# Routing of a mixture of experts moved between the tiles of the cross-attention's output projection, in a one-layer encoder

## The reference

```python
h = h + memory_cross_attention(rms_norm(h, norm_xatt), rms_norm(mem, mem_norm), wq, wk, wv, wo)  # 4 heads of 128
hn = rms_norm(h, norm_moe)
cl = hn @ w_coarse + b_coarse                    # 4 groups, the best one is taken
p_g, g = top_k(softmax(cl), 1)
top_v, top_i = top_k((hn @ w_fine)[group g] + b_fine, 2)   # 2 of its 8 experts
gate = softmax(top_v) * p_g
y = sum over the chosen experts e of (silu(hn @ w_gate[e]) * (hn @ w_up[e]) * gate) @ w_down[e]
out = rms_norm(h + y, final_norm)
```

## Time and profile before

| | us |
|---|---|
| median of three runs | 2049.28 |
| the profiled execution | 2048.28 |
| its span, first to last instruction | 2046.2 |
| PE, DVE, ACT, POOL busy in the span | 1825.2, 486.6, 398.4, 58.1 |
| DMA over the span | 247 GB/s |

### The profile page before, as it was taken

One profiled execution on the slowest core, in us unless ns is written; L12 is line 12 of the kernel. 1 busy time (PEld: TensorE's weight loads), 2 busy tenths in 40 slices (PEclk: granted clock), 3 DMA queues, 4 the chain that ended last, 5 costly groups with the idle time before them and its releaser, 6 DMA issues.

```text
span 2046.2 us, 29333 instructions
## 1 busy us (share of the span) xinstructions
PE 1825.2 (89%) x11998; PEld 1329.1 (65%) x11998; DVE 486.6 (24%) x1120; ACT 398.4 (19%) x1071; POOL 58.1 (3%) x100
## 2 busy tenths in 40 slices
PE   3999999999999999999769888999888899988882
PEld 3888888899988884467467554556555455655541
DVE  1101333777777741011320000000000000000003
ACT  2112221355555540012210000000000000000001
POOL 0000000000000000000000000000000000000000
PEclk9999999999999999999869999999999999999996
DMA  8832352200000045353218999999999999999993
GB/s 293 157 103 88 107 187 83 83 2 1 0 0 0 0 158 203 134 205 152 101 79 346 430 431 428 432 430 422 429 432 424 428 422 431 418 430 433 423 422 147
DMA packets 93357, 505.87 MB, mean 247 GB/s; under 512 B 39188, under 2 KB 43656, under 8 KB 74872
## 3 DMA queue, kind: packets, MB, share of 16 engines
q1 hardware_dynamic: 85456, 487.62, 58.7%
q0 software_dynamic: 6848, 14.12, 2.3%
q10 hardware_dynamic: 1000, 3.37, 0.6%
HBM read 498.76 MB, written 18.91 MB: 253 GB/s over the span
## 4 chain that ended last, share of the span: by engine, by line
PE 65%; DMA 27%; DVE 3%; ACT 2%; issue 1%; SPq 1%; DVEq 0%; ACTq 0%; POOLq 0%
DMA ring<-in_wu 26%; PE ps L1592 14%; PE ps L1233 13%; PE ps L1489 5%; PE ps L1406 4%; PE ps L1425 3%; PE ps L1631 3%; PE ps L1507 3%; PE ps L1582 3%; PE ps L1381 1%; PE ps L1431 1%; PE ps L1548 1%; PE ps L1516 1%; SPq L267 1%; PE ps L1213 1%
## 5 line engine op out<-in xcount | busy, mean ns | idle before, releaser
L1592 PE MATMUL ps<-ring,rkv 128*64 128x256 f32 x4096 | 477.0, 393 | 65.2 <-DMA ring<-in_wu 38.4
L1592 PEld LDWEIGHTS ps<-ring,rkv 128*64 128x64 f32 x4096 | 325.3, 142 | 226.2 <-DMA ring<-in_wu 49.6
L1233 PE MATMUL ps<-hnT,ring 128*128 128x256 f32 (+1 forms) x1280 | 282.2, 379 | 2.2 <-PE ps L1233 1.0
L1233 PEld LDWEIGHTS ps<-hnT,ring 128*128 128x128 f32 (+1 forms) x1280 | 239.1, 187 | 47.7 <-issue 10.2
L1631 PE MATMUL ps<-ring,gg 128*64 128x512 f32 x1024 | 240.1, 623 | 30.2 <-DMA ring<-in_wd 20.6
L1631 PEld LDWEIGHTS ps<-ring,gg 128*64 128x64 f32 x1024 | 83.3, 143 | 165.0 <-issue 141.7
L1177 DVE SCALAR_TENSOR_TENSOR gg<-ps,tmp,gg 128x256 f32<-128x256 f32 x32 | 15.5, 484 | 515.0 <-PE ps L1592 515.0
L1582 PE MATMUL ps<-hnT,sw 128*128 (+1 forms) x1024 | 120.8, 280 | 7.4 <-DVE hnT L1161 7.4
L1582 PEld LDWEIGHTS ps<-hnT,sw 128*128 128x128 f32 x1024 | 117.7, 195 | 13.3 <-issue 13.3
L1406 PE MATMUL ps<-ring 128*128 128x128 f32 x768 | 114.6, 275 | 0.1
L1406 PEld LDWEIGHTS ps<-ring 128*128 128x128 f32 x768 | 100.3, 192 | 0.7 <-ACT ring L558 0.3
(11 more groups left out here) (316 smaller groups left out, 1710.3 us busy)
## 6 DMA issues: line engine op xcount, KB each, us to landing
ring<-in_wg SPq DMA_DIRECT2D x32, 4096.0 KB, 20.1
ring<-in_wu SPq DMA_DIRECT2D x32, 4096.0 KB, 22.2
ring<-in_wd SPq DMA_DIRECT2D x32, 4096.0 KB, 18.0
ring<-in_w_in SPq DMA_DIRECT2D x7, 4096.0 KB, 15.1
ring<-in_w_out SPq DMA_DIRECT2D x4, 4096.0 KB, 13.9
ring<-in_w_in SPq DMA_DIRECT2D x16, 512.0 KB, 7.5
ring<-in_xatt_wk SPq DMA_DIRECT2D x1, 4096.0 KB, 13.5
ring<-in_xatt_wv SPq DMA_DIRECT2D x1, 4096.0 KB, 13.5
```

The lines of the kernel that those rows point to most:

```text
L1233: ins = mm(ps[0:rows_, m % 2, 0:T], lhs, hnT[:, k, :], start=k == 0, stop=k == KD - 1)
L1592: ins = mm(ps[CAP * h:CAP * h + CAP, bank, 0:T], xT[:, k, CAP * i:CAP * i + CAP], slot_k(slot)[:, k, T * h:T * h + T], start=k == 0, stop= ...
```

## The change

- Cross-attention goes head by head: the queries of head f are followed by the scores of head f - 1, the turning of head f - 2 and the values of head f - 3, two PSUM banks for each step. The output projection's first three tiles begin with the heads that are ready.
- Between the projection's tiles PE turns the rows of `tokA` as they are, unnormalised, and makes their logits four feature tiles at a time. The squares are taken by tiles of 512 too. The gain of `norm_moe` is multiplied into the router's weights; the row's 1/rms scales the logits when DVE reads them.
- The group and the experts are chosen by rank: how many others are larger (or equal and earlier), all pairs compared at once. The masks are built before the weights, so the counts run while the weights are made.
- The one-hots of experts 0 and 1 come before the loop, the others inside it.
- `select` reads raw rows of `tokA` with a step of 16 elements as the stationary operand. DVE evicts with the gain (`x_out` was ACT's). The row's 1/rms goes into the table as a third column: it scales the Silu's input and is part of the gate weight.
- `norm_moe` is one more row among the parameters and a small load by features; its broadcast load goes.

```diff
-ID, BO, MK, SU, ON, IO, SM, TV, DI, HB = 0, 128, 256, 768, 896, 1024, 1088, 1344, 1348, 1356
-NCST = 1357
-
-P_MIX, P_XATT, P_MEM, P_SP, P_SN = 0, 16, 32, 64, 94
+ID, BO, MK, SU, ON, IO, SM, TV, LT, HB, TH = 0, 128, 256, 768, 896, 1024, 1088, 1344, 1348, 1412, 1413
+NCST = 1417
+
+P_MIX, P_XATT, P_MEM, P_MOE, P_SP, P_SN = 0, 16, 32, 48, 64, 94
...
-    c[:, DI:DI + 8] = np.arange(8, 0, -1)
+    c[:, LT:LT + 64] = np.tri(8, k=-1).reshape(1, 64)
+    c[:, TH:TH + 4] = CAP * np.arange(4) - (np.arange(4) == 0)
...
-        xpT = hnT[:, 0:8, :].rearrange("p (h b) t -> p h b t", b=2)
-
-        gain_moe = memtok[:, 0, :]
+        xpT = sw[:, 0].rearrange("p (h b) t -> p h b t", b=2)
...
-        tab = tmp[:, 1400:1400 + 2 * NE].rearrange("p (j v) -> p j v", v=2)
+        tab = tmp[:, 1400:1400 + 3 * NE].rearrange("p (j v) -> p j v", v=3)
+        gain_moe = tmp[:, 1504:1504 + KD]
+        sqp = st[:, 40:48]
...
-            todo = [(0, r, by(a[name], P)) for r, name in ((P_MIX, "norm_mix"), (P_XATT, "norm_xatt"), (P_MEM, "mem_norm"))]
+            todo = [(0, r, by(a[name], P)) for r, name in ((P_MIX, "norm_mix"), (P_XATT, "norm_xatt"), (P_MEM, "mem_norm"), (P_MOE, "norm_moe"))]
...
-            for dst, g in ((gain_moe, "norm_moe"), (gain_fin, "final_norm")):
-                pool.dma_start(dst, bass.AP(tensor=a[g].tensor, offset=0, ap=[[0, P], [1, D]])).then_inc(S["gain_in"], 16)
+            pool.dma_start(gain_fin, bass.AP(tensor=a["final_norm"].tensor, offset=0, ap=[[0, P], [1, D]])).then_inc(S["gain_in"], 16)
             pool.wait_ge(S["xs_tr"], 4)
-            pool.dma_start(wr[:, :, 0:NG], a["wc"].rearrange("(p k) n -> p k n", p=P)).then_inc(S["route_in"], 16)
-            pool.dma_start(wr[:, :, NG:NR], a["wf"].rearrange("(p k) n -> p k n", p=P)).then_inc(S["route_in"], 16)
+            pool.dma_start(wr[:, :, 0:NG], a["wc"].rearrange("(k p) n -> p k n", p=P)).then_inc(S["route_in"], 16)
+            pool.dma_start(wr[:, :, NG:NR], a["wf"].rearrange("(k p) n -> p k n", p=P)).then_inc(S["route_in"], 16)
+            pool.dma_start(gain_moe, a["norm_moe"].rearrange("(p k) -> p k", p=P)).then_inc(S["route_in"], 16)
...
@@ scalar @@
+            for f in range(XH + 1):
+                if f < XH:
+                    queries(f)
+                if f >= 1:
+                    exp_head(f - 1)
+                if f >= 2:
+                    head_turned(f - 2)
+                if f >= 3:
+                    head_out(f - 3)
+            head_out(XH - 2)
+            head_turned(XH - 1)
+            head_out(XH - 1)
...
+            def row_squares(n):
+                b, q = n // 4, slice(F * (n % 4), F * (n % 4) + F)
+                act.wait_ge(S["xw_add"], n + 1)
+                A(tokB[:, b, q], tokA[:, b, q], ACT.Square, accum_out=sqp[:, n:n + 1]).then_inc(S["sq_done"], 1)
+
+            def rows_turned(n, c0=0):
+                act.wait_ge(S["r_tr"], n + 1)
+                b, k, bank = n // 4, 4 * (n % 4) + c0, TR_BANK[n] + c0 // 2
+                src = ps[:, bank, P * c0:4 * P].rearrange("p (k t) -> p k t", t=P)
+                A(hnT[:, k:k + 4 - c0, P * b:P * b + P], src, ACT.Copy).then_inc(S["r_ev"], 1)
+
+            def row_std(b):
                 act.wait_ge(S["var_done"], 5 + b)
                 A(stat(3, 2)[:, b:b + 1], stat(3, 1)[:, b:b + 1], ACT.Sqrt).then_inc(S["std_done"], 1)
-            turned(3)
+
+            row_squares(0)
+            row_squares(1)
+            for n in range(2, 7):
+                row_squares(n)
+                rows_turned(n - 2)
+                if n == 4:
+                    row_std(0)
+            rows_turned(5)
+            rows_turned(6)
+            row_squares(7)
+            rows_turned(7, 2)
+            row_std(1)
...
+                def job(e, first=False):
+                    j = b * NE + e
                     if first:
                         act.wait_ge(S["r_tab"], b + 1)
                         for h in range(2):
-                            ins = A(tab[CAP * h:CAP * h + CAP].rearrange("p j v -> p (j v)"), ps[0:CAP, 7, 0:2 * NE], ACT.Copy)
+                            ins = A(tab[CAP * h:CAP * h + CAP].rearrange("p j v -> p (j v)"), ps[0:CAP, 7, 0:3 * NE], ACT.Copy)
                         ins.then_inc(S["r_tabok"], 1)
-                    if then is not None:
-                        x_out(then)
+                        act.wait_ge(S["r_tabok"], b + 1)
+                    act.wait_ge(S["m_gate"], j + 2)
+                    act.wait_ge(S["m_hg"], j + 1)
+                    A(sil, ps[:, 0, 0:T], ACT.Silu, scale=tab[:, ds(e, 1), 2]).then_inc(S["m_sil"], 1)
...
@@ vector @@
-            def normed_moe(b):
-                dve.wait_ge(S["xw_add"], 4 * b + 4)
-                dve.wait_ge(S["sq_done"], 7 + b)
-                block_rstd(3, b, 5 + b)
-                dve.wait_ge(S["gain_in"], 32)
-                by_tile = tokB[:, b, :].rearrange("p (k q) -> p q k", k=KD)
-                V.scalar_tensor_tensor(by_tile, tokA[:, b, :].rearrange("p (q k) -> p q k", k=KD), stat(3, 2)[:, b:b + 1],
-                                       gain_moe.rearrange("p (q k) -> p q k", k=KD), ALU.mult, ALU.mult).then_inc(S["fin_h"], 1)
...
+            def row_rstd(b):
+                dve.wait_ge(S["sq_done"], 10 + 4 * b)
+                dc.link(V.tensor_reduce(stat(3, 0)[:, b:b + 1], sqp[:, 4 * b:4 * b + 4], AX.X, ALU.add))
+                block_rstd(3, b, 5 + b)
+
+            def logits(b):
+                dve.wait_ge(S["r_mm"], b + 1)
+                dc.add(V.scalar_tensor_tensor(lg[:, b], ps[:, 6 + b, 0:NR], stat(3, 2)[:, b:b + 1], rb, ALU.mult, ALU.add))
+
             for n in range(8):
                 b, q = n // 4, slice(F * (n % 4), F * (n % 4) + F)
                 dve.wait_ge(S["xw_mm"], n + 1)
-                V.tensor_tensor(tokA[:, b, q], tokA[:, b, q], ps[:, n, :], ALU.add).then_inc(S["xw_add"], 1)
-                if n == 7:
-                    normed_moe(0)
-
-
-            normed_moe(1)
-            turned(3)
-
-            def rs(o, n):
-                return rt[:, o:o + 2 * n].rearrange("p (b n) -> p b n", b=2)
-
-            def wide(x, n):
-                return x.broadcast_to([P, 2, n])
-
-            dve.wait_ge(S["r_mm"], 1)
-            dve.wait_ge(S["route_in"], 64)
-            lg = rs(0, NR)
-            dc.link(V.tensor_tensor(lg, ps[:, 0, 0:2 * NR].rearrange("p (b n) -> p b n", b=2),
-                                    rb.unsqueeze(1).broadcast_to([P, 2, NR]), ALU.add))
+                V.tensor_tensor(tokA[:, b, q], tokA[:, b, q], ps[:, WO_BANK[n], :], ALU.add).then_inc(S["xw_add"], 1)
+                if n == 1:
+                    dve.wait_ge(S["route_in"], 80)
+                    gains = prm[:, P_MOE:P_MOE + KD].unsqueeze(2).broadcast_to([P, KD, NR])
+                    V.tensor_tensor(wr, wr, gains, ALU.mult).then_inc(S["r_wr"], 1)
+                if n == 4:
+                    row_rstd(0)
+                if n == 6:
+                    logits(0)
+            dve.sem_inc(S["m_xe"], 2)
+            dve.wait_ge(S["r_tr"], 8)
+            V.tensor_copy(hnT[:, 12:14, P:2 * P], ps[:, 3, 0:2 * P].rearrange("p (k t) -> p k t", t=P)).then_inc(S["r_evv"], 1)
+            row_rstd(1)
+            logits(1)
...
+            def ranks(x, n, pairs, out_):
+
+                over = [P, 2, n, n]
+                mine, other = x.unsqueeze(3).broadcast_to(over), x.unsqueeze(2).broadcast_to(over)
+                dc.add(V.tensor_tensor(pairs[:, :, :, n:2 * n], other, mine, ALU.is_equal))
+                dc.add(V.tensor_tensor(pairs[:, :, :, 0:n], other, mine, ALU.is_gt))
+                dc.sync()
+                for b in range(TB):
+                    dc.add(V.tensor_tensor(pairs[:, b, :, n:2 * n], pairs[:, b, :, n:2 * n], before_[:, 0:n, 0:n], ALU.mult))
+                dc.sync()
+                dc.link(V.tensor_reduce(out_, pairs, AX.X, ALU.add))
...
+            ranks(cl, NG, pairs_of(NG), rank[:, :, 0:NG])
+            dc.link(V.tensor_scalar(goh, rank[:, :, 0:NG], 0.0, None, ALU.is_equal))
...
+            dc.link(V.tensor_reduce(fs, t32.rearrange("p b (g x) -> p b x g", g=NG), AX.X, ALU.add))
+            ranks(fs, EPG, pairs_of(EPG), rank)
+            oh1, oh2 = rs(204, EPG), rs(220, EPG)
+            both = rs(720, EPG)
+            dc.link(V.tensor_scalar(both, rank, 2.0, None, ALU.is_lt))
+            MM = rs(452, NE)
+            for b in range(TB):
+                ins = V.tensor_tensor(MM[:, b].rearrange("p (g x) -> p g x", g=NG),
+                                      goh[:, b].unsqueeze(2).broadcast_to([P, NG, EPG]),
+                                      both[:, b].unsqueeze(1).broadcast_to([P, NG, EPG]), ALU.mult)
+                if b:
+                    ins.then_inc(S["r_pos"], 1)
+                else:
+                    dc.add(ins)
...
+            def one_hot(t, lo, hi):
+                pb = pos[:, t, lo:hi].unsqueeze(2).broadcast_to([P, hi - lo, CAP])
```

(132 more changed lines are left out.)

198 lines of the change are left out of this document (81 added, 117 removed).

## The result

The kernel after takes 2091.26 us (median of four runs, 2087.67 to 2098.31) against 2049.14 for the kernel before (median of four). The ratio is 1.0208, 95% interval 1.0196 to 1.022: slower by 42 us, where 2026 was forecast. The profiled execution took 2087.67 us, its span is 2085.4, the granted clock 0.979.

The account below looks back on a forecast made before the run. The DMA stream of expert weights bounds the kernel, and work ahead of gate 0 delays its start. 2048.28 - 22.7 + 0.2 = 2025.8, stated as 2026, range 2019 to 2072.

Parts of the forecast that it names:

- From the queries to the logits: Queries start at 934.4; logits ready near 1011.6 instead of 1029.0, 17.4 gained, as other products fill PE's waits.
- logits to block count: Masks come first, out at 1016.0; block count at 1019.6 instead of 1040.0.
- block count to gate 0: Selection starts at 1020.9 instead of 1045.9, waits for DVE (free 1029.1); gate 0 at 1033.7, 22.7 gained in all.
- The strided stationary: Selection's loads of tokA columns 64 bytes apart taken at the floor: 192 ns long, 7.34 us for 64.
- rival 1: Strided load slows the selection to 14.8 us, weight slots free late: loss 9 to 52, total 2038 to 2081; chance 0.31.
- The other end: Upper price of the strided load, from DVE's L706 at 1.81 ns each: 0.23 us a load, selection 14.8 us.
- Reading is not writing: Argument against a slow strided load in the selection: its price came from DVE's L706, which writes 512 bytes apart.
- After that: Gate 0 through up 0 stays at 26.3; small later delays are hidden; parameter rows cost 0.2.
- 6.9 us of cover: Expert stage: PE needs 52.8 of 59.7 us per two experts, so a 0.3 delay of down is hidden.
- Rivals 2 and 3: 2: front gains less (comparisons, clock), 2032 to 2038, chance 0.12; 3: stream hides front, no change, 0.05 with the rest.

Follow-up runs that it names:

- contiguous version: Kernel after, but the selection loads 128 neighbouring columns of tokA (gathers wrong features): 2025.31 us, ratio 0.9887 to the kernel before.
- cut version: Kernel after, still step 16, selection cut in two: two quarters behind the even expert's up product, two behind the odd's; 2035.5 us, ratio 0.9933.

## Why the prediction was wrong

*From the queries to the logits; logits to block count; block count to gate 0.* Right, within 1.1 us at every point: logits 1012.7 (forecast 1011.6), PE's counts 1016.76 (1016.0), block count 1020.1 (1019.6), selection 1021.36 (1020.9), DVE free for the evictions at 1028.95 (1029.1). With contiguous loads gate 0 came at 1033.01 (1033.7) and the total at 2025.31 (2025.8). Of the 1.1 us at the logits, 0.9 was there before they began: the queries started at 935.33, not at 934.4.

*The strided stationary.* This is the step that failed. The floor of 192 ns and 7.34 us a selection was taken, since the nearest row was the step-2 load. That row lies on the other side of the stair: in this very instruction a step of 2 costs almost nothing (197 ns, 7.80 us), but at 16 bytes and more the load takes 312 to 335 ns and the selection 14.2 to 15.5. The choice by nearness was the error. Between 8 bytes and 64 the row said nothing, and the rule of the Trainium skill that rival 1 names (SBUF — State Buffer, the note on cachelines in "Door 1: The DMA port swizzle"), two hits per line, did. The other end, 14.8 us from DVE's write, came close by luck: it carried a write of DVE, 512 bytes apart, over to a load of TensorE, and no run ties the two together. "Reading is not writing" did not help: DVE's own copy with this step of reading took 595 ns where a copy of long runs takes 417. One number can mislead: the threshold of "a load of 0.197 us" in rival 1 is a distance from load to load (12.6 us / 64), while the 197 ns measured at step 2 is the duration of one record. Records overlap, and the distance there is 7.80 / 64 = 0.122 us; at step 16 it is 0.222.

*After that.* Gate 0 to the end of up 0 "stay at 26.3": so it was with contiguous loads (1033.01 to 1059.40), but the kernel after took 24.8, since the granted clock was 0.86 there instead of 0.81. "6.9 us of cover" added up PE's busy time over the pair. That the sum fits is not the condition: the cut version is busy 811 of 850 us and has a full stream, and the kernel after is busy less (778) and has not. The condition is the longest distance between two slot releases. For the small delay of DVE's evictions, 0.3 us, the cover held (the contiguous version's longest distance is 15.6, DMA share 1.00).

*Rival 1.* It is what happened, with the right mechanism: a slot freed late. Its condition was "a selection under 11.3 us"; at 14.2 that gives 2.9 us a pair, at its own 14.8 it gave 3.5, and 3.95 was measured. So the term "what is late per pair" was about 1 us too small at the real selection. The window of 2 us at half share, in which the stream comes back, is as large; that it is the reason was not tested. Its sign was half right: the DMA share fell below 0.97, but PE waited for `wu` (36.6 us), not for `wd`. Its front gain of 19.7 was 19.6 at gate 0 and 21.2 at the first `wu`. Its end of 52 was the better one, and 59 was the loss. The low end, 9, came from PE's throughput; by the same sum a selection of 14.2 gives 52.8 + 6.9 = 59.7 us, just the period of the stream and no loss, and the cut version bears that out (59.6). Its middle "about 2064" is not the middle of 2038 to 2081, which is 2060. The stated range ended at 2072, below this rival's own upper end, and the measured 2091 lies beyond both.

*Rivals 2 and 3.* Not seen: the wide comparisons and the sum behind them took 0.42 us at most, the clock was 1.00 in the second half of the contiguous version's first selection, behind the wait, and the front's gain went through to the end.

## What to carry to other kernels

Before a strided view is given to TensorE as the stationary operand, look at the bytes between its columns: for f32, two elements apart cost next to nothing in this selection (197 ns against 192), and four, eight and sixteen apart took 1.6 to 1.7 times as long. If the data is needed in another order, let the engine that is idle reorder it once, outside the loop. DVE pays for such a copy too, but once for each element and not in every pair of experts.

For a stream through a ring of slots, the measure of cover is the longest time between two releases against what the other slots still hold, not the busy sum of the period. Here a long piece of work, cut and laid in two places, cost the stream nothing; moved whole, it moved the hole.
